# A trunk of two decoder layers: the weights' rounded parts of 22 pieces a layer come by casting transfers, their remainders two pieces later, and the mask is preset in all heads but the first

## What is computed

```python
for l in range(DEPTH):
    h = h + 0.5 * swiglu(rmsnorm(h, ffn1_norm[l]), ffn1_w_gu[l], ffn1_w_down[l])
    h = h + mixer(rmsnorm(h, mix_norm[l]), w_in[l], ret_gn[l], w_ret_proj[l],
                  w_sb_proj[l], w_out[l], pos, valid)
    h = h + 0.5 * swiglu(rmsnorm(h, ffn2_norm[l]), ffn2_w_gu[l], ffn2_w_down[l])
h = rmsnorm(h, final_norm)
```

```python
z = jnp.einsum('bhqd,bhkd->bhqk', q_blk, kf) * scale
log_1mb = jnp.where(mask, jax.nn.log_sigmoid(-z), 0.0)
acc = lax.cumsum(log_1mb, axis=3, reverse=True) - log_1mb
a = jnp.where(mask, jnp.exp(jax.nn.log_sigmoid(z) + acc), 0.0)
```

## Time and profile before

| | us |
|---|---|
| median of 3 runs | 1289.12 (1289.07 to 1289.5) |
| the profiled execution | 1289.24 |
| its span, first to last instruction | 1287.4 |
| PE busy | 1279.5 (99%) |
| DVE busy | 875.7 (68%) |
| ACT busy | 703.6 (55%) |
| POOL busy | 55.6 (4%) |
| DMA: 219.3 MB, mean | 170 GB/s |

### The profile page before, as it was taken

How to read it: one execution, slowest core, us unless ns; L and a number is a source line. 1 busy time by engine, 2 the same in 40 slices (tenths; PEclk the granted TensorE clock), 3 DMA queues, 4 the chain that set the end, 5 groups by cost and what they waited for, 6 DMA issues and landing times.

```text
span 1287.4 us, 26188 instructions
## 1 busy us (share of the span) xinstructions
PE 1279.5 (99%) x10302; PEld 1274.4 (99%) x10302; DVE 875.7 (68%) x1103; ACT 703.6 (55%) x955; POOL 55.6 (4%) x48
## 2 busy tenths in 40 slices
PE   9999999999999999999999999999999999999998
PEld 8999999999999999999999999999999999999998
DVE  7766556878777776665576665568788877766653
ACT  6444446757777554444454444467678775544442
POOL 2000001000000010000010000010000000100000
PEclk9999999999999999999999999999999999999999
DMA  7655554554344555555545555545543445655552
GB/s 295 211 173 171 179 178 150 190 168 135 126 137 147 167 179 178 172 177 174 180 159 185 179 173 173 178 164 180 176 136 132 146 152 178 197 188 183 184 180 82
DMA packets 60705, 219.30 MB, mean 170 GB/s; under 512 B 6864, under 2 KB 6992, under 8 KB 60496
## 3 DMA queue, kind: packets, MB, share of 16 engines
q1 hardware_dynamic: 60192, 217.27, 50.8%
q10 hardware_dynamic: 432, 0.85, 0.2%
HBM read 217.04 MB, written 1.05 MB: 169 GB/s over the span
## 4 chain that ended last, share of the span: by engine, by line
PE 98%; DVE 1%; ACT 1%; DMA 0%; issue 0%; DVEq 0%; ACTq 0%
PE bank L1176 31%; PE bank L1178 31%; PE bank L1177 31%; PE bank L1332 1%; PE bank L1424 1%; PE bank L1321 1%; PE bank L1304 0%; PE bank L1462 0%; DMA raw<-stream 0%; PE bank L1457 0%; PE bank L1339 0%; PE bank L1131 0%; DVE w_lo L698 0%; PE bank L1322 0%; PE bank L1135 0%; PE bank L1133 0%
## 5 line engine op out<-in xcount | busy, mean ns | idle before, releaser
L698 DVE TENSOR_TENSOR w_lo<-raw,w_hi 128x1024 fp32r<-128x1024 f32 x407 | 510.6, 1261 | 262.5 <-ACT w_hi L423 257.3
L1176 PE MATMUL bank<-xh,w_hi 128*128 128x272 f32 (+1 forms) x2224 | 641.2, 288 | 0.0
L423 ACT ACTIVATE w_hi<-raw 128x1024 fp32r<-128x1024 f32 x407 | 427.8, 1057 | 381.4 <-PE bank L1178 380.4
L1178 PE MATMUL bank<-xh,w_lo 128*128 128x272 f32 (+1 forms) x2224 | 635.9, 286 | 0.0
L1177 PE MATMUL bank<-xl,w_hi 128*128 128x272 f32 (+1 forms) x2224 | 635.5, 286 | 0.0
L1177 PEld LDWEIGHTS bank<-xl,w_hi 128*128 128x128 f32 x2224 | 418.6, 188 | 0.0
L1176 PEld LDWEIGHTS bank<-xh,w_hi 128*128 128x128 f32 x2224 | 418.3, 188 | 0.0
L1178 PEld LDWEIGHTS bank<-xh,w_lo 128*128 128x128 f32 x2224 | 418.0, 188 | 0.0
L1178 PE MATMUL bank<-gh,w_lo 128*128 128x272 f32 (+1 forms) x1016 | 290.9, 286 | 0.0
L1176 PE MATMUL bank<-gh,w_hi 128*128 128x272 f32 (+1 forms) x1016 | 290.5, 286 | 0.0
L1177 PE MATMUL bank<-gl,w_hi 128*128 128x272 f32 (+1 forms) x1016 | 289.7, 285 | 0.0
(11 more groups left out here) (213 smaller groups left out, 750.2 us busy)
## 6 DMA issues: line engine op xcount, KB each, us to landing
raw<-stream SPq DMA_DIRECT2D x407, 512.0 KB, 3.3
table<-tables SPq DMA_DIRECT2D x1, 1424.0 KB, 8.7
out<-rv_gb SPq DMA_DIRECT2D x3, 256.0 KB, 2.6
gain_h<-tokens SPq DMA_DIRECT2D x2, 272.0 KB, 6.4
raw<-stream SPq DMA_DIRECT2D x2, 256.0 KB, 4.5
rv_gb<-squares SPq DMA_DIRECT2D x1, 384.0 KB, 8.2
gain_h<-tokens ACTq DMA_DIRECT2D x1, 300.0 KB, 4.3
gain_h<-tokens ACTq DMA_DIRECT2D x1, 272.0 KB, 5.2
```

Source lines behind the costliest of these rows:

```text
L423: eng.activation(w_hi[:, slot, :], raw[:, slot, :], ACT.Copy).then_inc(hi_ready, 1)
L698: eng.tensor_tensor(w_lo[:, slot, :], raw[:, slot, :], w_hi[:, slot, :].bitcast(F32), ALU.subtract).then_inc(lo_ready, 1)
L1176: pe.matmul(out, wh, hi, start=first, stop=False)
L1178: mm = pe.matmul(out, wl, hi, start=False, stop=last)
```

## The change

Three things change. First, for the mixer's steps 24 to 45 (`CAST`) POOL issues a transfer from DRAM into `w_hi` that casts float32 to float32r on its way (`cast_hi`), when piece s is done; ACT no longer rounds these 22 pieces. SP still loads them to `raw`, since DVE needs them for the remainder. Second, the remainder of a cast piece is made two steps later (`due`, `split_cast`): steps 24 and 25 make none, step 26 makes that of 24, and step 47 makes those of 45, 46 and 47. POOL's copies for the tails are set between its casts: the second keys after the cast of step 28, the last queries after that of step 35. Third, `KEPT_MASKS` falls from 3 to 1: heads 1 and 2 lose the mask matmul and get ACT's mask copy. `hi_ready` counts fewer roundings, so `split_lo` takes off the casts made before. The diff:

```diff
@@ -82,7 +82,9 @@
 STACKED = HEADS // 2
-KEPT_MASKS = 3
+KEPT_MASKS = 1
+CAST = range(24, 46)
+CAST_LAG = 2
 OUT_TOK = [N_META, N_META + P]
@@ -258,6 +260,14 @@
+        def casts_before(l, s):
+            return l * len(CAST) + len([c for c in CAST if c < s])
+        def cast_count(l, s):
+            return len([c for c in CAST if c % RING == s % RING]) * l + len([c for c in CAST if c % RING == s % RING and c <= s])
         def layers(layer):
@@ -265,6 +275,7 @@
         raw_ready = [sem(f"raw_ready{i}") for i in range(RING)]
+        hi_in = [sem(f"hi_in{i}") for i in range(RING)]
         hi_ready, lo_ready, piece_done = sem("hi_ready"), sem("lo_ready"), sem("piece_done")
@@ -369,7 +380,7 @@
                     if i == 2:
-                        place_queries(l)
+                        mixer(l)
                     for p in range(1, PAIRS):
@@ -385,17 +396,36 @@
-            def place_queries(l):
+            def cast_hi(l, s):
+                n, slot = l * PER_LAYER + FFN + s + RING, (FFN + s) % RING
+                pool.wait_ge(piece_done, n - (RING - 1))
+                pool.dma_start(w_hi[:, slot, :], stream[n]).then_inc(hi_in[slot], 16)
+            def mixer(l):
+                place_first_keys(l)
+                for s in CAST:
+                    cast_hi(l, s)
+                    if s == 2 * U_SK + 4:
+                        place_second_keys(l)
+                    if s == 2 * U_SQ[1] + 1:
+                        place_last_queries(l)
+            def place_first_keys(l):
                 pool.wait_ge(ssum_done, l * 3 + 2)
...
                 pool.wait_ge(rq_tail_in, l + 1)
+            def place_second_keys(l):
                 pool.wait_ge(ret_tail_scores, l + 1)
...
                 pool.wait_ge(key_tail_ready, 2 * l + 2)
+            def place_last_queries(l):
                 pool.wait_ge(unit_evicted, evicted(l, U_SQ[1]))
@@ -507,7 +537,8 @@
                         take_h(l * 3 + 2, (s - S_OUT) // 2, qf)
-                    split_hi(base + (s + RING), (FFN + s) % RING)
+                    if s not in CAST:
+                        split_hi(base + (s + RING), (FFN + s) % RING)
                     u = s // 2
@@ -692,9 +723,20 @@
         def _(eng):
-            def split_lo(n, slot):
-
-                eng.wait_ge(hi_ready, n + 1)
+            def split_lo(n, slot, casts=0):
+                eng.wait_ge(hi_ready, n + (1 - casts))
+                remainder(slot)
+            def split_cast(l, s):
+                slot = (FFN + s) % RING
+                eng.wait_ge(hi_in[slot], 16 * cast_count(l, s))
+                eng.wait_ge(raw_ready[slot], (l * PER_LAYER + FFN + s + RING - slot) * (16 // RING) + 16)
+                remainder(slot)
+            def remainder(slot):
                 eng.tensor_tensor(w_lo[:, slot, :], raw[:, slot, :], w_hi[:, slot, :].bitcast(F32),
@@ -765,6 +807,7 @@
                 last = first_query(l) > 0 and f == 1
+                casts = casts_before(l + f, 0)
                 q0 = first_query(l) if f else 0
@@ -779,7 +822,7 @@
                 def next_lo(it, j):
-                    split_lo(base + it * 4 + (j + RING), (off + j) % RING)
+                    split_lo(base + it * 4 + (j + RING), (off + j) % RING, casts)
@@ -824,7 +867,7 @@
                             if not last or n + RING < FFN:
-                                split_lo(base + (n + RING), (off + n) % RING)
+                                split_lo(base + (n + RING), (off + n) % RING, casts)
@@ -1031,8 +1074,18 @@
-                    for n in [] if s == MIX - 2 else [s - 1, s] if s == MIX - 1 else [s]:
-                        split_lo(base + (n + RING), (FFN + n) % RING)
+                    def due(s):
+                        if CAST.start <= s < CAST.stop + CAST_LAG:
+                            late = [s - CAST_LAG] if s - CAST_LAG in CAST else []
+                            return late + (list(range(CAST.stop, s + 1)) if s == CAST.stop + CAST_LAG - 1 else [])
+                        return [] if s == MIX - 2 else [s - 1, s] if s == MIX - 1 else [s]
+                    for n in due(s):
+                        if n in CAST:
+                            split_cast(l, n)
+                        else:
+                            split_lo(base + (n + RING), (FFN + n) % RING, casts_before(l, n))
```

## The result

The changed kernel takes 1293.22 us (median; 1293.11 to 1293.69) where the kernel before, run beside it, takes 1289.24 us (1289.04 to 1289.5). The ratio is 1.0031, with a 95% interval of 1.0022 to 1.0040: slower by 4.0 us. The forecast was 1292.5.

The account below looks back on a forecast made before the run. The prediction took PE's work to bound the kernel. +3.8 us for the three remainders in step 47 and -0.5 for the masks, all else 0, gave +3.3 on 1289.24: 1292.5 us, range 1290.0 to 1297.0.

Parts of the forecast that it names:

- What bounds the kernel: PE, busy 1279.5 of 1287.4 us and idle 0.1 of 165 beside the heads; removing ACT's roundings is directly worth 0.
- Rival C: Beside the heads: records hide PE time that ACT's rounding costs, so not slower, 1285.9 to 1290.3 us; chance 6%.
- The step that costs: Step 47: three remainders in a row shift DVE's chain by 1.92 and 1.88 us; +3.8 us for both layers.
- rival D: Step 47: the late chain costs less than its shift, as DVE is earlier; 1290.5 to 1291.7 us; chance 12%.
- The cast transfer: Steps 24 to 45: lands in about 4 us, at most 7.9, with 8.1 available; rate 1.57 us; cost 0.
- rival A: Cast steps: casts too slow in rate, 3.1 us of the sixteen engines each; about 1323 us; chance 9%.
- Issuing on POOL: Issuing a cast takes POOL about 1 us, with at least 1.78 left before the tail queries are read; cost 0.
- Rival B: POOL's issue waits out DVE's remainders, taking 2.5 to 3.5 us; tail queries late; 1293.5 to 1296.5 us; chance 16%.
- The moved copy of the second keys: POOL's copy moves from step 27 behind the cast of step 28; PE needs it some 30 us later; cost 0.
- The masks: Heads 1 and 2: four mask matmuls less, net 0.12 us each, -0.5 us; ACT's copies hidden by 0.6 us.
- Tight remainder of step 42: Its end at 361.29 would serve the piece starting at 361.54; about 0.4 us left with earlier ACT work; cost 0.
- The head start of ACT's chain: In the heads, without the rounding (1.06 us) and with a mask copy (0.52), ACT's chain starts about 0.5 us sooner.

Follow-up runs that it names:

- e1: The kernel before with only the late remainders (45, 46 and 47 in step 47), no casts, masks as before: 1292.8 us against 1289.07, ratio 1.0029.
- e5: The changed kernel with the remainder of piece 45 put ahead of DVE's wait for piece 47, two left behind it: 1290.84 us, ratio 1.0014.
- e3: The changed kernel with piece 45's remainder ahead of DVE's wait in step 47 and piece 48's in idle time of step 49: 1289.27 us, ratio 1.0002.
- e9: The changed kernel with each cast issued one piece later, POOL's two other copies one cast earlier: 1296.38 us, ratio 1.0062.
- e12: The changed kernel with remainders one step late instead of two, so no queue of three: 1291.61 us, ratio 1.0018.
- e4: The changed kernel with POOL's copy of the second keys behind the cast of step 27 instead of 28: 1292.82 us.
- e11: The changed kernel with KEPT_MASKS = 3, so casts and late remainders but the masks of heads 1 and 2 as products: 1293.57 us.
- e2: The kernel before with KEPT_MASKS = 1 and nothing else: 1289.8 us against 1289.07, ratio 1.0007.

## Why the prediction was right, point by point

**What bounds the kernel.** Right: 44 roundings less on ACT brought no PE time. Only the busy share was read too strictly. PE had one short wait beside the heads in each layer that it doesn't show; the waits from 349 to 351.5 us (total, times, longest) have that of layer 0, before and then in the changed kernel:

```profile
PEld bank L1321 <- DVE gl L912: 0.2, 1, 0.2
...
PEld bank L1374 <- DVE gl L955: 0.4, 1, 0.4
```

It becomes a term further down. Rival C falls by its own sign: the distance between the first two matmuls of a piece, averaged over steps 25 to 45, is 0.19 us before and after in both layers, and in the changed trace the steps 30 to 38 are as long as before to 0.02 us.

**The step that costs.** Right in place, cause and size. The shift was forecast at 1.92 and 1.88 us; measured are 1.81 (L943 at 380.99 against 379.14, and piece 48 0.04 us later) and about 1.8. The prediction took 3.42 us for three remainders, they need 3.40, and piece 47's handover was a little quicker. e1 makes the loss without transfers, and e5 and e3 take it away by parts and wholly. By steps the loss is 3.6 us where 3.8 was forecast. That nothing of it comes back was right too, against rival D.

**The cast transfer.** Latency forecast 0, with a budget of 8.1 us and 7.9 as the upper bound: the longest took 7.4, the median 4.7 (4 forecast), and no DVE wait for a landing appears. e9 and e12, with about 4 us less, show waits at once: without the second piece of lag some casts come late. Rate: forecast 1.57 us, like a load, measured 1.79. That is under the limit of 2.4 us (2.3 by the shorter pieces of layer 1) and far from the 3.1 of rival A; the DMA share of 0.82 confirms that both fit.

**Issuing on POOL.** Forecast about 1 us, range 0 to a few: measured 0.53. Rival B had POOL wait until DVE's remainders are over. The timelines of POOL and DVE of the changed kernel have an issue that lies wholly inside one:

```profile
291.94 1.23 DVE L740 TENSOR_TENSOR w_lo<-raw,w_hi 128x1024 fp32r<-128x1024 f32 x1 [1.27 <-PE bank L1231]
...
292.20 0.53 POOL L403 DMA_DIRECT2D w_hi<-stream  x1 [3.17 <-PE bank L1231]
```

There are six such, all of 0.53 us, so the rival falls. The rule that the prediction cited is for DVE's two-port modes. The same page of the Trainium skill (SBUF — State Buffer, Who interferes with whom) says that a subtraction of two tensors has none; the trace agrees, and the citation was the wrong rule for this instruction. The right one, on two inputs from SBUF, stands beside it and points at the second keys.

**The moved copy of the second keys: the step that failed.** The prediction looked at when PE needs the copy ("some 30 us later, so 0") and forgot whom it meets on the way. It had the row that shows it: 1.50 us for a remainder beside this very copy. Its own "0 to 0.3 us on some remainders, inside the slack" was true of the old place and false of the new one. Cost 0.32 us, shown by e4.

**The masks.** Forecast -0.5, measured -0.48 by steps beside the casts (e11), while the two traces alone seem to say 0.2. The term missing is a different one: **the casts lengthen step 41 by 0.14 us a layer**, 0.28 in all, since two of ACT's instructions follow each other less closely where the rounding has gone (read from the traces; no run changes this distance alone). The prediction set the removal of a rounding at 0 or better and did not look at L912 in step 41 as a wait that PE already had. That the copies are hidden "by 0.6 us" is true of PE, which waits for none of them; but where ACT still rounds they push a rounding back, and that costs more than the masks give (e2).

**Tight remainder of step 42.** Right: e1 costs 0.12 there in layer 1, the changed kernel 0. The head start of ACT's chain in layer 0 was 0.36 us (its first instruction on the scores at 354.32 instead of 354.68), where the prediction took 0.5.

**Step 54.** Not foreseen, +0.36 us. It goes with a load of instructions, and its cause is open.

The sum from the experiments' terms: queue +3.6, keys +0.32, step 41 +0.28, step 54 +0.36, masks -0.48, is +4.1; measured +4.0; forecast +3.3. The time came out close because the one large term was right. Three terms of together 0.96 us were put at nothing, and the queue, taken 0.2 too dear, hid a part of that; with a smaller main term these omissions would have decided the forecast.

## What to carry to other kernels

Relief for an engine is worth what the bounding engine waits for it, and here that was next to nothing; what a change costs lies where work deferred for its sake is paid back. Pay such a debt where the paying engine already waits for something (two remainders in DVE's idle time cost 0, in the queue 3.6 us). When an operation moves, ask not only when its result is due, but which instruction of another engine it will run beside and who waits for that one.

## What was not expected of the hardware

- How much a POOL copy and DVE subtractions lengthen each other where they overlap: 0.61 us became 1.05 and 1.62 for the copy of 128x512, 0.43 became 0.85 for 128x272, and 1.23 became 1.52 for a remainder.
- A casting transfer of 512 KB from POOL takes 1.79 us of the sixteen engines against 1.64 for a load, lands in 3.5 to 7.4 us (median 4.7 against 3.4), and its issue occupies POOL for 0.53 us, inside a DVE instruction too.
- One DVE instruction of 226 started 0.35 us late in nine of the ten kernels with casts, each time the same one, and each time a load of instructions of 8192 bytes began 0.7 to 1.0 us behind that start; 16 idle waits earlier in the program moved the load by 11.5 us and removed the delay.
